# Residual additions on VectorE alone, modulation rows behind the products, and the first output granule by bank pairs

## The chip, the cores and the metric

One core of a Trainium2 chip runs the whole program in one launch. The metric is the time of one execution on the device, in microseconds (us). TensorE is written PE (matmuls) and PEld (weight loads), VectorE is DVE, ScalarE is ACT, GpSimd is POOL, and SyncE is SP.

## The reference, cut to what matters

Two blocks of two layers each work on 256 tokens of width 1024; everything is fp32. The first block also carries 256 context tokens beside the 256 latent ones. What the change touches is this part of the reference:

```python
def rms_norm(x, g):
    return x * lax.rsqrt(jnp.mean(x * x, axis=-1, keepdims=True) + EPS) * g

def swiglu(u, wi, wo):
    g, up = jnp.split(u @ wi, 2, axis=-1)
    return (jax.nn.silu(g) * up) @ wo
...
    m = (jax.nn.silu(c) @ w_ada + b_ada).reshape(c.shape[0], 1, N_MOD, D_MODEL)   # modulation, w_ada: 1024 x 9216 a layer
    mc = (jax.nn.silu(c_ctx) @ w_ada + b_ada).reshape(1, 1, N_MOD, D_MODEL)

    def pre(t, mm, i, gi):
        return rms_norm(t, g[gi]) * (1 + mm[:, :, i + 1]) + mm[:, :, i]

    def post(t, y, mm, i, gi, wres):
        return t + wres * mm[:, :, i + 2] * rms_norm(y, g[gi])
...
    h = post(h, swiglu(pre(h, m, 0, 0), ffn_wi[0], ffn_wo[0]), m, 0, 1, 0.5)      # first feed-forward
    h = post(h, o @ w_o, m, 3, 3, 1.0)                                            # mixer
    h = post(h, swiglu(pre(h, m, 6, 4), ffn_wi[1], ffn_wo[1]), m, 6, 5, 0.5)      # second feed-forward
# second block: x = x + _rmsnorm(mixer(...), g1);  x = x + _rmsnorm(_conv_ffn(_rmsnorm(x, g2), ...), g3)
```

## The kernel before, in words

Activations lie transposed: the model width is on the partitions, in 8 parts of 128 (`KD` = 8), and the tokens lie along the free axis, `T` = 512 (latent and context together) for most of the first block, 256 for the rest. `h[:, k, :]` is the residual stream of part k.

Every product is made from split operands: a weight tile is copied to its high part by ACT (L438), its low part is the difference, made by DVE (L443), and `multiply` (L445) issues three matmuls for each product (L452 to L454: high by high, high by low, low by high). Weights come through a ring of two 2 MB slots that SP loads (L408); one split step of 128 x 2048 is a granule, and there are two buffers each for the high and low parts.

The stages run one after another, each a block with one instruction list for each engine:

- `setup` (L497) loads the tokens, transposes them into `h`, loads six tiles of `w_ada` (1.5 MB each), multiplies them with the two conditioning vectors (`ada_rows`, L638, matmuls of L644), and makes the first norm's sum of squares. ACT squares each part of `h` (L623), and PE adds the eight with eight matmuls against a matrix of ones (L558), between the modulation tiles. The transposes of the vectors that are needed late (L565) stand at PE's end, and DVE's copies of them (L574) at DVE's end.
- `ffn1` (L1228), four times, is a feed-forward of 22 granules (`KF` = 22). `pair_products` (L1186) makes the gate and the value of granule g, 48 matmuls; ACT takes the gate (L1266), DVE multiplies (L1286) and so frees the banks, counted in `dve_free`. In the first two `ffn1` stages with a `w_ada` load (those of layer 0) the remaining 42 modulation tiles are made beside the products, one in a granule: class `Ada` (L667) loads a tile from ACT's queue into one single slot (L681), PE multiplies it (`Ada.rows`, L697), and only then can ACT issue the next load. `rows(0)` stands behind the first granule's products; for every later granule `rows(g)` stands in front of its products. The first stage has 22 such tiles, the second 20.
- `Down` (L1027) is the output product of the same feed-forward, 11 granules of 48 matmuls that add up in all eight PSUM banks. Granule 0 of it starts when its banks come free: before the first matmul into a bank, PE waits for the `dve_free` count of the granule whose gate or value lay there. The order is all eight banks for the first half of the granule (kk = 0), then all eight for the second (kk = 1). `ffn2` (L2069) uses the same `Down` behind a feed-forward with a short convolution, whose last step frees the banks (L2135).
- `Residual` (L877) with `Norm` (L731) is the border between two stages, ten times in all (one of them without a norm behind it). One matmul with ones gives the sum of squares of the new branch (L945), ACT makes 1/sqrt in `rstd` (L938, L939), DVE multiplies the eight parts with it (L954 where T is 512, L956 where T is 256), and the products are added to `h`: the odd parts by DVE (L961), the even ones by POOL (L966). ACT squares each new part (L771), PE sums the eight squares with eight matmuls with ones (L801), ACT makes the next `rstd` (L775, L776), DVE scales `h` (L807 or L809). Where T is 512 ACT then applies gain and shift in two instructions a part (L755, `make`) and copies the high part `uh` (L783), and DVE makes the low part `ul` (L816), which the first product waits for.

Each engine runs its list in order; a wait blocks all that is behind it on that engine.

Of the kernel before, what the change touches and what calls it, by code (L numbers as in the profile page):

```python
# [31 lines left out]
P = 128  # L32
D = 1024
# [126 lines left out]
def two_blocks(nc, a, out, stop=None):  # L160
    ctx = ExitStack()
    with ctx:
# [96 lines left out]
        def col(name, i, n=1):  # L259
# [17 lines left out]
        sum_ready, h_squared, h_updated, h_updated2, h_scaled, u_made, u_high, u_ready, gains = (signal(n) for n in (  # L277
            "norm_sum_ready", "h_squared", "h_updated_by_vector", "h_updated_by_gpsimd", "h_scaled", "input_made",
# [15 lines left out]
        first_loaded, late_loaded, tokens_loaded, const_loaded, gain_loaded, x_squared, x_summed = (signal(n) for n in (  # L294
            "first_vectors_loaded", "late_vectors_loaded", "tokens_loaded", "const_loaded", "gains_loaded", "x_squared", "x_summed"))
# [201 lines left out]
        def setup():  # L497
# [14 lines left out]
            SQUARES = {2: (0, 1), 3: (2, 3, 4), 4: (5, 6, 7)}  # L512
            TOKENS = {0: (0, 1, 2), 1: (3, 4, 5), 2: (6, 7)}

            with stage() as block:
# [18 lines left out]
                def _(pe):  # L534
# [8 lines left out]
                    for i in range(ADA_FIRST):  # L543
# [17 lines left out]
                    pe.wait_ge(late_loaded.sem, late_loaded.at(16 * len(late)))  # L561
                    for t in range(EARLY, len(row_tiles)):
                        g, m = KD + t, row_tiles[t]
                        turned(g)
                        pe.transpose(ps[:, bank_of(g), 0:m], rows[0:m, t, :], ident[0:m, 0:m]).then_inc(prod.sem, 1)  # L565

                @block.vector
                def _(dve):
# [9 lines left out]
                    for i in range(ADA_FIRST):  # L578
                        for j in TOKENS.get(i, ()):
                            g = EARLY + j  # L580
                            dve.wait_ge(prod.sem, prod.at(g + 1))
                            dve.tensor_copy(h[:, j, :], ps[:, bank_of(g), :]).then_inc(dve_free.sem, 1)
# [3 lines left out]
                    dve.wait_ge(gain_loaded.sem, gain_loaded.at(16 * 8))  # L586
                    dve.tensor_scalar(head_gain[:, 0::2], head_gain[:, 0::2], HD ** -0.5, None, ALU.mult)
                    for t in range(EARLY, len(row_tiles)):
                        take_cols(KD + t, t)

                @block.scalar
                def _(act):
# [21 lines left out]
                    for i in range(ADA_FIRST):  # L614
                        if i == ADA_FIRST - 1:
                            act.wait_ge(x_summed.sem, x_summed.at(KD))
                            act_chain.link(act, act.activation(rstd[:, :], ps[:, 7, :], ACT.Ln, scale=1.0 / D, bias=eps[:, 0:1]))
                            act.activation(rstd[:, :], rstd[:, :], ACT.Exp, scale=-0.5)
                        for k in SQUARES.get(i + 1, ()):
                            act.wait_ge(dve_free.sem, dve_free.at(EARLY + k + 1))  # L620
                            if k >= 4:
                                act.wait_ge(x_summed.sem, x_summed.at(k - 3))
                            act.activation(sq[:, k % 4, :], h[:, k, :], ACT.Square).then_inc(x_squared.sem, 1)  # L623
# [107 lines left out]
        class Norm:  # L731
# [26 lines left out]
            def scalar(self, act, high_of):  # L758
# [4 lines left out]
                else:  # L763
                    self.post.scalar(act)
                    for k in range(KD):

                        if k % 2:
                            act.wait_ge(h_updated.sem, h_updated.at(k // 2 + 1))
                        else:
                            act.wait_ge(h_updated2.sem, h_updated2.at(k // 2 + 1))  # L770
# [69 lines left out]

            def gpsimd(self, pool):
                if self.post is not None:
                    self.post.gpsimd(pool)
# [33 lines left out]
        class Residual:  # L877
# [69 lines left out]
            def vector(self, dve):  # L947
                T = self.T
                dve.wait_ge(y_rstd.sem, y_rstd.at(1))
                for k in range(KD):  # L950
# [8 lines left out]
                    if k % 2:  # L959
# [3 lines left out]
            def gpsimd(self, pool):  # L963
                for k in range(0, KD, 2):
                    pool.wait_ge(y_part.sem, y_part.at(k + 1))
# [32 lines left out]
        def residual(r):  # L998

            with stage() as block:  # L1000
# [12 lines left out]
                @block.gpsimd  # L1013
                def _(pool):
                    r.gpsimd(pool)
# [2068 lines left out]
```

## Time and profile before

| | |
|---|---|
| median of 3 runs | 3060.27 us (3059.58 to 3060.49) |
| the profiled execution's own time | 3062.88 us |
| its span | 3061.0 us |
| mean granted clock of TensorE over the span | 0.937 |
| busy: PE, PEld, DVE, ACT, POOL | 2780.4, 2356.8, 1342.7, 1176.4, 85.5 us |
| HBM read | 372.33 MB, 122 GB/s over the span |

The span runs from the first to the last instruction of the program in one profiled execution; 1.9 us of that execution lie outside it. An engine is busy while an instruction of it runs. The granted clock is 1.00 at full speed (2.4 GHz) and 0.50 at the lower level (1.2 GHz). In a row of the timeline "[4.62 <-ACT arena L771]" means that the engine had been idle for 4.62 us and that ACT's instruction of line 771 ended the wait.

### The profile page before, as it was taken

What the parts mean: (1) busy time and instruction counts of PE and PEld (TensorE: products, weight loads), DVE (VectorE), ACT (ScalarE), POOL (GpSimd) and SP (SyncE); (2) the same over time, 40 slices, a digit from 0 to 9 for tenths busy, and PEclk for the clock granted to TensorE, in tenths of its full rate; (3) what the DMA queues carried; (4) which work ended last, traced back from release to release, by engine and by line L of the source; (5) the groups of instructions that cost most, each with busy time, mean ns of one, the idle gap of its engine ahead of it and who ended that gap; (6) DMA issues with size and microseconds to landing.
All of it is one profiled execution on the core that took longest, in us unless ns stands there. A gap on an engine that the chain in (4) does not pass through costs nothing. (4 is left out here: it accounts for less than half of the span.)

```text
span 3061.0 us, 40121 instructions
## 1 busy us (share of the span) xinstructions
PE 2780.4 (91%) x16888; PEld 2356.8 (77%) x16888; DVE 1342.7 (44%) x1618; ACT 1176.4 (38%) x1581; POOL 85.5 (3%) x118
## 2 busy tenths in 40 slices
PE   5899998998999997999989899798896999777998
PEld 3677786875677785887868799798765899777998
DVE  3122236464222235222365644455445575444664
ACT  3122225444222225222254544343324464333653
POOL 3000000000000003000000000000000000000000
PEclk8899999999999998999999899899967899878899
DMA  8666321203566223232222355354000454331452
GB/s 278 197 206 206 145 95 63 77 29 103 185 212 213 101 98 86 82 110 82 96 83 62 105 165 177 115 190 142 1 1 28 138 190 154 117 106 56 138 171 104
DMA packets 277180, 375.54 MB, mean 123 GB/s; under 512 B 11020, under 2 KB 232696, under 8 KB 276912
## 3 DMA queue, kind: packets, MB, share of 16 engines
q1 hardware_dynamic: 228288, 300.56, 29.3%
q10 hardware_dynamic: 46576, 69.26, 6.7%
q0 software_dynamic: 2176, 3.67, 0.8%
q8 instruction: 109, 1.79, 0.2%
q14 instruction: 31, 0.25, 0.0%
HBM read 372.33 MB, written 1.16 MB: 122 GB/s over the span
## 5 line engine op out<-in xcount | busy, mean ns | idle before, releaser
L452 PE MATMUL ps<-uh,wh 128*128 128x256 f32 (+1 forms) x4224 | 1415.7, 335 | 70.7 <-DVE ul L816 31.0
L453 PE MATMUL ps<-ul,wh 128*128 128x256 f32 (+1 forms) x4224 | 1400.0, 331 | 0.0
L454 PE MATMUL ps<-uh,wl 128*128 128x256 f32 (+1 forms) x4224 | 1398.4, 331 | 0.0
L452 PEld LDWEIGHTS ps<-uh,wh 128*128 128x128 f32 x4224 | 813.5, 193 | 188.6 <-issue 82.3
L443 DVE TENSOR_TENSOR wl<-ring,wh 128x2048 fp32r<-128x2048 f32 x212 | 482.2, 2274 | 941.5 <-ACT wh L438 834.4
L454 PEld LDWEIGHTS ps<-uh,wl 128*128 128x128 f32 x4224 | 813.4, 193 | 72.8
L453 PEld LDWEIGHTS ps<-ul,wh 128*128 128x128 f32 x4224 | 814.0, 193 | 69.6 <-issue 0.7
L438 ACT ACTIVATE wh<-ring 128x2048 fp32r<-128x2048 f32 x156 | 298.4, 1913 | 803.7 <-PE ps L454 737.3
L1059 DVE TENSOR_TENSOR wl<-ring,wh 128x2048 fp32r<-128x2048 f32 x66 | 151.3, 2292 | 334.0 <-ACT uh L1077 296.9
L1056 ACT ACTIVATE wh<-ring 128x2048 fp32r<-128x2048 f32 x66 | 126.3, 1914 | 350.1 <-PE ps L454 350.1
L966 POOL TENSOR_TENSOR h<-h,arena 128x256 f32<-128x256 f32 (+1 forms) x40 | 43.7, 1093 | 2825.0 <-DVE arena L954 1441.4
L1478 ACT ACTIVATE wh<-ring 128x2048 fp32r<-128x2048 f32 (+2 forms) x38 | 70.0, 1842 | 125.9 <-PE ps L454 125.9
L801 PE MATMUL ps<-arena,const 128*128 128x256 f32 (+1 forms) x144 | 76.7, 699 | 38.7 <-ACT arena L771 38.7
L801 PEld LDWEIGHTS ps<-arena,const 128*128 128x128 f32 x144 | 39.0, 288 | 77.7 <-ACT arena L771 64.7
L644 PE MATMUL ps<-arena,act_c 128*32 128x384 f32 x736 | 72.8, 515 | 26.7 <-DMA arena<-in_w_ada_dram 26.7
L452 PE MATMUL ps<-wh,uh 128*128 128x256 f32 (+2 forms) x288 | 84.4, 293 | 0.0
L454 PE MATMUL ps<-wh,ul 128*128 128x256 f32 (+2 forms) x288 | 82.0, 285 | 0.0
L453 PE MATMUL ps<-wl,uh 128*128 128x256 f32 (+2 forms) x288 | 82.0, 285 | 0.0
L1084 DVE TENSOR_TENSOR ul<-arena,uh 128x1024 fp32r<-128x1024 f32 (+1 forms) x66 | 62.8, 952 | 28.1 <-ACT uh L1077 28.1
L1636 ACT ACTIVATE arena<-ps,softs 128x512 f32<-128x512 f32 (+1 forms) x72 | 43.6, 613 | 77.7 <-DVE softs L1675 62.6
L2152 DVE SCALAR_TENSOR_TENSOR arena<-ps,cols,arena 128x255 f32<-128x255 f32 x176 | 72.5, 473 | 0.0
L644 PEld LDWEIGHTS ps<-arena,act_c 128*32 128x32 f32 x736 | 19.9, 112 | 63.7 <-issue 50.8
(295 smaller groups left out, 2288.5 us busy)
## 6 DMA issues: line engine op xcount, KB each, us to landing
ring<-in_ffn_wi_dram SPq DMA_DIRECT2D x88, 1024.0 KB, 7.7
arena<-in_w_ada_dram ACTq DMA_DIRECT2D x42, 1536.0 KB, 6.6
ring<-in_ffn_w_up_dram SPq DMA_DIRECT2D x44, 1024.0 KB, 7.2
ring<-in_ffn_wo_dram SPq DMA_DIRECT2D x20, 2048.0 KB, 7.9
ring<-in_ab_w_in_dram SPq DMA_DIRECT2D x13, 2048.0 KB, 7.8
ring<-in_ffn_w_down_dram SPq DMA_DIRECT2D x10, 2048.0 KB, 7.8
ring<-in_c_w_in_dram SPq DMA_DIRECT2D x6, 2048.0 KB, 8.0
ring<-in_w_in_dram SPq DMA_DIRECT2D x20, 512.0 KB, 6.0
```

The lines of the kernel that those rows point to most:

```text
L438: act.activation(shape_of(wh[b]), raw, ACT.Copy).then_inc(high.sem, 1)
L443: dve.tensor_tensor(shape_of(wl[b]), raw, shape_of(wh[b]), ALU.subtract).then_inc(split.sem, 1)
L452: pe.matmul(to, sh, mh, start=start and n == 0, stop=False)
L453: pe.matmul(to, sh, ml, start=False, stop=False)
L454: mm = pe.matmul(to, sl, mh, start=False, stop=stop and last)
L644: last = pe.matmul(ps[q:q + 32, bank, 0:ADA_COLS], act_c[:, kk, ds(30 - 2 * r, 32)], weights[:, kk, :], start=(first and kk < 4), stop=(en ...
L801: last = pe.matmul(self.sum_bank(), ones, self.sq[:, k, :], start=(k == 0), stop=(k == KD - 1))
L1056: return act.activation(wh[side(self.key, g)][:, :], self.weights(g), ACT.Copy)
L1059: return dve.tensor_tensor(wl[side(self.key, g)][:, :], self.weights(g), wh[side(self.key, g)][:, :], ALU.subtract)
L1084: dve.tensor_tensor(to_l, of, to_h, ALU.subtract).then_inc(split.sem, 1)
L1478: act.activation(shaped(wh[side(key, g)]), raw, ACT.Copy).then_inc(high.sem, 1)
L2152: ins = dve.scalar_tensor_tensor(out=conv_buf[:, q, part, to], in0=ps[:, 2 * q + part, of], scalar=channel("ffn_conv_w", tap, part, g), in ...
```

## The change

Five edits, all in the order of work; no product, load or element-wise result is added or left out except where named.

1. `pair_products`: `rows(g)` moves behind the products of granule g. The tiles are shared out as 21 and 21 instead of 22 and 20, so that the last granule has none.
2. `Down.tensor`: every granule but the last goes by pairs of banks, both halves kk of a pair before the next pair; in granule 0 each pair waits once, before its first matmul.
3. `Residual` and `Norm`: POOL's four additions of each border go to DVE. DVE multiplies part k and then adds part k - 1.
4. `Norm.scalar`, T = 512: the high copy of part 0 is made before gain and shift of part 1.
5. `setup`: the eight squares are added by DVE (seven instructions of 128 x 512), and PE sums once; the late vectors are transposed and copied before the last modulation tile is done.

```diff
# setup
-                        for k in SQUARES.get(i, ()):
-                            if k == 0:
-                                pe.wait_ge(const_loaded.sem, const_loaded.at(16))
-                            pe.wait_ge(x_squared.sem, x_squared.at(k + 1))
-                            pe.matmul(ps[:, 7, :], ones, sq[:, k % 4, :], start=(k == 0), stop=(k == KD - 1)).then_inc(x_summed.sem, 1)
+                        if i == SUM_AFTER:      # 3
+                            pe.wait_ge(const_loaded.sem, const_loaded.at(16))
+                            pe.wait_ge(x_added.sem, x_added.at(KD - 1))
+                            pe.matmul(ps[:, 7, :], ones, sq_of(0), start=True, stop=True).then_inc(x_summed.sem, 1)
+                        if i == LATE_AFTER:     # 4
+                            pe.wait_ge(late_loaded.sem, late_loaded.at(16 * len(late)))
+                            for t in range(EARLY, len(row_tiles)):
+                                g, m = KD + t, row_tiles[t]
+                                turned(g)
+                                pe.transpose(ps[:, bank_of(g), 0:m], rows[0:m, t, :], ident[0:m, 0:m]).then_inc(prod.sem, 1)
...
+                    def add_square(k):
+                        dve.wait_ge(x_squared.sem, x_squared.at(k + 1))
+                        if k > 1:
+                            dve.wait_ge(x_added.sem, x_added.at(k - 1))
+                        dve.tensor_tensor(sq_of(0), sq_of(0), sq_of(k), ALU.add).then_inc(x_added.sem, 1)
+
+                    for j in range(KD):
+                        g = EARLY + j
+                        dve.wait_ge(prod.sem, prod.at(g + 1))
+                        dve.tensor_copy(h[:, j, :], ps[:, bank_of(g), :]).then_inc(dve_free.sem, 1)
+                        if j >= 2:
+                            add_square(j - 1)
+                    add_square(KD - 1)
+                    for t in range(EARLY, len(row_tiles)):
+                        take_cols(KD + t, t)
...
# Norm.scalar, T = 512
                     self.make(act, 0)
                     for k in range(KD):
-                        if k + 1 < KD:
+                        if 0 < k < KD - 1:
                             self.make(act, k + 1)
                         act.wait_ge(u_made.sem, u_made.at(2 * (k + 1)))
                         act.activation(uh[:, k, 0:T], self.made[:, k, :], ACT.Copy).then_inc(u_high.sem, 1)
+                        if k == 0:
+                            self.make(act, 1)
...
# Residual.vector (Residual.gpsimd and every block's POOL list with it are taken out)
-                    if k % 2:
-                        dve.wait_ge(y_part.sem, y_part.at(k + 1))
-                        dve.tensor_tensor(h[:, k, 0:T], h[:, k, 0:T], self.y[:, k, :], ALU.add).then_inc(h_updated.sem, 1)
+                    if k:
+                        self.update(dve, k - 1)
+                self.update(dve, KD - 1)
+
+            def update(self, dve, k):
+                dve.wait_ge(y_part.sem, y_part.at(k + 1))
+                dve.tensor_tensor(h[:, k, 0:self.T], h[:, k, 0:self.T], self.y[:, k, :], ALU.add).then_inc(h_updated.sem, 1)
...
# Down.tensor
-                left = {6: (dve_free, KF - 2), 0: (dve_free, KF - 1), 2: (dve_free, KF)}
-                order = (6, 7, 0, 1, 4, 5, 2, 3)
+                left = [((4, 5), dve_free, KF - 3), ((6, 7), dve_free, KF - 2), ((0, 1), dve_free, KF - 1), ((2, 3), dve_free, KF)]
                 if self.ada is not None:
-                    left, order = {0: (dve_free, KF - 1), 2: (dve_free, KF), 6: (ada_summed, 2)}, (4, 5, 0, 1, 2, 3, 6, 7)
+                    left = [((4, 5), ada_copied, 2), ((0, 1), dve_free, KF - 1), ((2, 3), dve_free, KF), ((6, 7), ada_summed, 2)]
...
-                        for kk in range(2):
-                            for j in order:
-                                if g == 0 and kk == 0 and j in left:
-                                    sem, count = left[j]
-                                    pe.wait_ge(sem.sem, sem.at(count))
-                                c = slice(kk * D + j * P, kk * D + (j + 1) * P)
-                                last = multiply(pe, ps[:, j, 0:self.T], [((vh[:, c], vl[:, c]), (xh[:, kk, :], xl[:, kk, :]))],
-                                                start=(g == 0 and kk == 0), stop=False)
+                        for banks, free, count in left:
+                            if g == 0:
+                                pe.wait_ge(free.sem, free.at(count))
+                            for kk in range(2):
+                                for j in banks:
+                                    c = slice(kk * D + j * P, kk * D + (j + 1) * P)
+                                    last = multiply(pe, ps[:, j, 0:self.T], [((vh[:, c], vl[:, c]), (xh[:, kk, :], xl[:, kk, :]))],
+                                                    start=(g == 0 and kk == 0), stop=False)
...
# pair_products
                 pe.wait_ge(free.sem, free.at(g + 1 - pairs))
-                if ada is not None:
-                    ada.rows(pe, g)
...
                 last.then_inc(prod.sem, 1)
+                if ada is not None:
+                    ada.rows(pe, g)
...
-        adas = {(0, 0): Ada(tiles[:KF]), (0, 1): Ada(tiles[KF:])}
+        adas = {(0, 0): Ada(tiles[:KF - 1]), (0, 1): Ada(tiles[KF - 1:])}
```

## Rows read from the trace of the kernel before

**Rows 1.** The page's first part, busy time of each engine.
```profile
PE 2780.4 (91%) x16888; PEld 2356.8 (77%) x16888; DVE 1342.7 (44%) x1618; ACT 1176.4 (38%) x1581; POOL 85.5 (3%) x118
```

**Rows 2.** Waits of PE, whole span: line waited for: us in total, times, longest.
```profile
PE ps L801 <- ACT arena L771: 38.7, 20, 4.6
...
PE ps L644 <- DMA arena<-in_w_ada_dram: 26.7, 3, 15.5
...
PE ps L452 <- DVE arena L2135: 8.6, 2, 4.3
...
PE ps L452 <- DVE arena L1286: 2.2, 3, 1.3
```

**Rows 3.** Timeline of PE, both stages with modulation rows: start, us, instruction [idle before].
```profile
87.37 2.79 PE L644 MATMUL ps<-arena,act_c 128*32 128x384 f32 x16 [15.47 <-DMA arena<-in_w_ada_dram]
...
102.71 1.50 PE L644 MATMUL ps<-arena,act_c 128*32 128x384 f32 x16
...
115.28 1.50 PE L644 MATMUL ps<-arena,act_c 128*32 128x384 f32 x16
...
772.13 2.79 PE L644 MATMUL ps<-arena,act_c 128*32 128x384 f32 x16 [6.80 <-DMA arena<-in_w_ada_dram]
...
786.49 1.50 PE L644 MATMUL ps<-arena,act_c 128*32 128x384 f32 x16
```

**Rows 4.** Timeline of ACT, then line L681's landing times to 100 us and after 85 us.
```profile
72.10 0.40 ACTq L681 DMA_DIRECT2D arena<-in_w_ada_dram  x1
...
DMA to landing us min/median/max: 6.7/10.7/15.1
...
DMA to landing us min/median/max: 6.3/6.6/7.4
```

**Rows 5.** Timeline of PE and of DVE where the first second-block output product starts.
```profile
2555.41 0.58 PE L452 MATMUL ps<-uh,wh 128*128 128x256 f32 x1 [4.32 <-DVE arena L2135]
...
2554.94 0.99 DVE L2135 TENSOR_TENSOR arena<-arena 128x256 f32<-128x256 f32 x2
```

**Rows 6.** Busy time by stretch there: length, PE, PEld, DVE, ACT, POOL, granted clock, DMA.
```profile
2554.40:2561.10 6.70, 5.69 (x26) 5.70 (x27) 2.07 (x5) 2.33 (x3) 0.00 (x0) 0.50 0.28 70
2561.20:2568.00 6.80, 6.80 (x59) 6.80 (x59) 2.23 (x2) 2.44 (x2) 0.00 (x0) 1.00 0.58 235
```

**Rows 7.** Timeline of DVE, POOL, ACT, PE at the 484 us border, T = 512.
```profile
483.80 1.29 DVE L954 TENSOR_TENSOR arena<-arena,rstd 128x512 f32<-128x512 f32 x2 [2.20 <-ACT rstd L939]
485.13 1.63 DVE L961 TENSOR_TENSOR h<-h,arena 128x512 f32<-128x512 f32 x1
...
498.96 1.89 DVE L807 TENSOR_TENSOR arena<-h,rstd 128x512 f32<-128x512 f32 x3 [1.37 <-ACT rstd L776]
...
493.20 1.65 POOL L966 TENSOR_TENSOR h<-h,arena 128x512 f32<-128x512 f32 x1 [1.23 <-DVE arena L954]
...
494.87 1.18 ACT L771 ACTIVATE arena<-h 128x512 f32<-128x512 f32 x2 [1.70 <-POOL h L966]
...
486.93 8.29 PE L801 MATMUL ps<-arena,const 128*128 128x512 f32 x12 [4.62 <-ACT arena L771]
495.56 1.98 PE L801 MATMUL ps<-arena,const 128*128 128x512 f32 x4 [0.33 <-ACT arena L771]
```

**Rows 8.** Busy time by stretch in the same border, columns as in Rows 6.
```profile
492.00:494.00 2.00, 2.00 (x5) 1.07 (x5) 1.97 (x4) 1.18 (x3) 0.80 (x1) 0.83 0.00 0
```

**Rows 9.** Timeline of PE at the 1737 us border, T = 256.
```profile
1741.74 4.20 PE L801 MATMUL ps<-arena,const 128*128 128x256 f32 x10 [0.66 <-ACT arena L771]
```

**Rows 10.** Timeline of ACT and of PE behind the 731 us border, T = 512.
```profile
748.87 0.62 ACT L783 ACTIVATE uh<-arena 128x512 fp32r<-128x512 f32 x1
...
750.35 0.77 PE L452 MATMUL ps<-uh,wh 128*128 128x512 f32 x1 [5.61 <-DVE ul L816]
```

**Rows 11.** Timeline of DVE and of ACT at the end of setup.
```profile
48.61 1.08 DVE L574 COPY cols<-ps 128x128 f32<-128x128 f32 x5
...
50.82 1.91 ACT L438 ACTIVATE wh<-ring 128x2048 fp32r<-128x2048 f32 x1 [3.62 <-DMA ring<-in_ffn_wi_dram]
```

More of the change, by code:

```diff
@@ L275, in two_blocks @@
         aux = signal("second_dve_step")
-        sum_ready, h_squared, h_updated, h_updated2, h_scaled, u_made, u_high, u_ready, gains = (signal(n) for n in (
-            "norm_sum_ready", "h_squared", "h_updated_by_vector", "h_updated_by_gpsimd", "h_scaled", "input_made",
+        sum_ready, h_squared, h_updated, h_scaled, u_made, u_high, u_ready, gains = (signal(n) for n in (
+            "norm_sum_ready", "h_squared", "h_updated", "h_scaled", "input_made",
             "input_high_parts", "input_ready", "gains_ready"))
@@ L293, in two_blocks @@
             "ada_tile_loaded", "ada_tile_multiplied", "ada_rows_copied", "ada_columns_made", "ada_columns_summed", "ada_columns_taken"))
-        first_loaded, late_loaded, tokens_loaded, const_loaded, gain_loaded, x_squared, x_summed = (signal(n) for n in (
-            "first_vectors_loaded", "late_vectors_loaded", "tokens_loaded", "const_loaded", "gains_loaded", "x_squared", "x_summed"))
+        first_loaded, late_loaded, tokens_loaded, const_loaded, gain_loaded, x_squared, x_added, x_summed = (signal(n) for n in (
+            "first_vectors_loaded", "late_vectors_loaded", "tokens_loaded", "const_loaded", "gains_loaded", "x_squared", "x_squares_added", "x_summed"))
         ada_ready = [signal(f"ada_tile{i}_loaded") for i in range(ADA_FIRST)]
@@ L511, in setup @@
             bank_of = lambda g: 4 + g % 3
-            SQUARES = {2: (0, 1), 3: (2, 3, 4), 4: (5, 6, 7)}
+            SUM_AFTER, LATE_AFTER = 3, 4
+            sq_of = lambda k: sq[:, 1 + (k - 1) % 3, :] if k else sq[:, 0, :]
             TOKENS = {0: (0, 1, 2), 1: (3, 4, 5), 2: (6, 7)}
@@ L577, in _ @@
                         take_cols(t, t)
[L578 to L582, printed above, removed]
+                    def add_square(k):
[12 more added lines that the diff above has]
+                        take_cols(KD + t, t)
+                    dve.wait_ge(gain_loaded.sem, gain_loaded.at(16 * 8))
+                    dve.tensor_scalar(head_gain[:, 0::2], head_gain[:, 0::2], HD ** -0.5, None, ALU.mult)
                     dve.wait_ge(ada_turned.sem, ada_turned.at(1))
@@ L585, in _ @@
                     ada_take(dve, mod_sums, 0, ADA_FIRST).then_inc(ada_taken.sem, 1)
[L586 to L589, printed above, removed]
                 @block.scalar
@@ L613, in _ @@
                     act.preload_act_table_set(LN_EXP)
[L614 to L623, printed above, removed]
+                    for k in range(KD):
+                        act.wait_ge(dve_free.sem, dve_free.at(EARLY + k + 1))
+                        if k >= 4:
+                            act.wait_ge(x_added.sem, x_added.at(k - 3))
+                        act.activation(sq_of(k), h[:, k, :], ACT.Square).then_inc(x_squared.sem, 1)
+                    act.wait_ge(x_summed.sem, x_summed.at(1))
+                    act_chain.link(act, act.activation(rstd[:, :], ps[:, 7, :], ACT.Ln, scale=1.0 / D, bias=eps[:, 0:1]))
+                    act.activation(rstd[:, :], rstd[:, :], ACT.Exp, scale=-0.5)
                     act.wait_ge(ada_multiplied.sem, ada_multiplied.at(ADA_FIRST))
@@ L958, in vector @@
                     ins.then_inc(y_part.sem, 1)
-                    if k % 2:
-                        dve.wait_ge(y_part.sem, y_part.at(k + 1))
-                        dve.tensor_tensor(h[:, k, 0:T], h[:, k, 0:T], self.y[:, k, :], ALU.add).then_inc(h_updated.sem, 1)
-            def gpsimd(self, pool):
-                for k in range(0, KD, 2):
-                    pool.wait_ge(y_part.sem, y_part.at(k + 1))
-                    pool.tensor_tensor(h[:, k, 0:self.T], h[:, k, 0:self.T], self.y[:, k, :], ALU.add).then_inc(h_updated2.sem, 1)
-                pool.wait_ge(h_updated2.sem, h_updated2.at(KD // 2))
+                    if k:
[4 more added lines that the diff above has]
+                dve.tensor_tensor(h[:, k, 0:self.T], h[:, k, 0:self.T], self.y[:, k, :], ALU.add).then_inc(h_updated.sem, 1)
             def tail_done(self):
@@ L979, in done @@
                 y_part.passed(KD)
[L980 to L981 removed]
+                h_updated.passed(KD)
         def residual1(l, i, gi, weight, T=T2):
@@ L1296, in _ @@
                 def _(pool):
-                    norm.gpsimd(pool)
                     if bands_of is not None:
@@ L1487, in _ @@
                     steps(split_one, lambda g: take(dve, 1, dve_free, g), beside.vector(dve) if beside else lambda g: None)
-                @block.gpsimd
-                def _(pool):
-                    norm.gpsimd(pool)
             norm.done()
@@ L1746, in _ @@
                         stream(sp, out_key)
-                @block.gpsimd
-                def _(pool):
-                    norm.gpsimd(pool)
                 @block.tensor
@@ L2163, in _ @@
                     down.vector(dve)
-                @block.gpsimd
-                def _(pool):
-                    norm.gpsimd(pool)
             norm.done()
```

17 lines of the change are left out of this document (1 added, 16 removed).

## The prediction

> **What bounds the kernel now.** I read the busy times first. PE is busy for 2780 of 3061 us [rows 1], and every product and load stays, so the change can only give back part of the 281 us in which PE idles, and what PE loses at the lower clock behind such idle time. Next, the waits of PE by releaser, to see which idle time the five edits touch [rows 2]: 38.7 us before the sums of squares (L801), 26.7 us for modulation tiles, 8.6 us and 2.2 us before banks at the start of `Down`. Then the timeline at each of these places. PE is the only engine that is never covered there, so a microsecond won on PE's list is one won of the end.
>
> **Edit 1, rows behind the products.** In the first stage PE waits 15.47 us, from 71.90 to 87.37, for tile 1; in the second 6.80 us [rows 3]. The cause is the order: ACT can issue load 1 only behind `rows(0)`, at 72.10, it lands 15.1 us later (the longest of the three loads to 100 us) [rows 4], and `rows(1)` stands next on PE with nothing between. After the change granule 1's 48 matmuls stand between. One granule with its rows is 12.57 us (102.71 to 115.28) and the rows are about 1.45 of it, so the products are 11.1 us. Load 1 is issued as before and should land at 87.2; PE does products until 83.0 and waits 4.3 us: 11.1 us less. The clock comes on top: from `rows(1)` to `rows(2)` PE took 15.34 us instead of 12.57, 2.8 us lost; in the second stage 14.36, 1.8 lost [rows 3], each behind its wait. I charge the 4.3 us that stay with the 1.8 us that the 6.80 us wait cost. First stage: 11.1 + 2.8 - 1.8 = 12.1. Second stage: the load has 11.1 us of cover for a wait of 6.80, so 6.8 + 1.8 = 8.6. Together **20.7 us** (18 if the clock gives nothing back and load 1 comes no later; 22.5 if the short wait costs no clock). Moving a tile from the first stage to the second is 1.45 us from one to the other.
>
> What is queued behind the new wait: ACT waits for `rows(g)`, then issues the next load, splits granule g + 2 (1.9 us), takes the gate of g (0.6); DVE makes the low part (2.3 us). Granule g + 2 starts 11.1 + 1.45 us behind `rows(g)`, and the chain is under 5 us (L438's 1.91 us as in [rows 11]), so 7 us are free. Load g + 1 has 11.1 us of cover, as before, and takes 6.6 us, 7.4 at most [rows 4].
>
> **Edit 2, `Down` by pairs.** Before, PE did 6 matmuls (banks 6 and 7, first half) and waited 4.32 us for bank 0, freed by DVE's second last product (L2135) [rows 5]; there are two such waits [rows 2]. Now banks 4, 5, 6 and 7 are free already and give 24 matmuls before that wait. 18 matmuls at 0.12 us (59 in 6.80 us [rows 6]) move into the idle time: 2.1 us. Behind the wait the granted clock was 0.50 for 6.8 us and 26 matmuls took 5.7 us, 2.7 more than at full clock [rows 6]. The idle time shrinks to 2.2 us, so I expect the fall to be gone in most cases, and take 4.0 each, **8.0** for two (4.2 to 9.6). What is late next is the low part of granule 1's input, behind the second L2135 of the pair that ends at 2555.9 [rows 5], one ACT table load and one copy, an estimated 2 us: about 2558, just when granule 0 now ends (2555.4 and 24 matmuls). The three waits for L1286, 2.2 us, go whole [rows 2]: where T is 512 there are 12 more matmuls (0.23 us each) of cover for 0.4 us, where T is 256 there are 18 more for 1.3 us. **2.2**. The later granules change only the order of banks: 0.
>
> **Edit 3, additions on DVE.** At the 484 us border, T = 512, DVE's multiplications go in 1.29 us a pair, and its addition takes 1.63 us; the last POOL addition ends at 494.85, ACT squares two parts behind it, and PE's last two sums end at 497.54 [rows 7]. On one engine it is 16 instructions. The trace has no such addition without POOL beside it. From below it is L807 (h by rstd, both from SBUF), three in 1.89 us, 0.605 each; from above the 1.63 us itself. I take 0.605: the same shape and operands, and the 1.63 us end 0.55 us behind POOL's. Then part 6 is added at 483.80 + 14 x 0.605 + 0.68 = 492.95 and part 7 at 493.56, squared by 494.2 instead of 496.05: 1.9 us earlier. PE's sums may be later: they start at 486.4 instead of 486.93, the clock is at half until about 492.7 (0.83 over 492 to 494 [rows 8]), a part costs about 1.75 us at half and 0.9 at full clock, so 3.6 parts and then 4.4 x 0.9 gives 496.7: 0.9 us gained. The four borders with T = 512 lie between 0.9 and 1.9 each, according to when the clock rises; 1.4 on the mean, **5.6** (2 to 9, if the clock rises earlier or later).
>
> The Trainium skill (SBUF — State Buffer, section Who interferes with whom) says that a VectorE instruction with two SBUF inputs and a GpSimd instruction that reads SBUF exclude each other, the later one blocked until the first ends. That reads the 1.63 us as about 1.0 of waiting and 0.6 of work, and the sum by it is the 5.6 above; if the 1.63 were the addition's own price, the sum would be that of rival E.
>
> At T = 256 I count **0** (-1.5 to 1.5 over the five): PE's last five parts take 4.20 us without a break [rows 9], PE is the pace, and ACT's split of a granule stands between parts 2 and 3 as before. The last border, without a norm, ends with DVE's sixteenth instruction either way: 0.
>
> **Edit 4, first high part.** `uh` of part 0 starts at 748.87 behind four `make` instructions and PE's first product at 750.35 [rows 10]. Two of the four now stand behind it, 1.0 us earlier. The later parts come no sooner, since ACT's work is the same, and PE is at half clock there, so about half of it counts: 0.45 at two borders, **0.9** (0 to 2). Where PE has other work in the gap (the two `latent` borders) and at setup, where DVE splits weights first: 0.
>
> **Edit 5, setup.** The five copies of the late vectors, 1.08 us, leave DVE's end. But ACT's first split waited for its ring tile until 50.82 (3.62 us idle, released by the DMA) [rows 11], which neither PE nor DVE can bring sooner. **0** (-1, if the modulation load issued earlier takes from the ring tile; +1.4).
>
> **Sum.** 20.7 + 8.0 + 2.2 + 5.6 + 0.9 = 37.4 us off the profiled execution's own 3062.9 us (3061.0 span and 1.9 around it) gives 3025.5. The median of the runs is 2.6 us below that execution: **3023 us**. Where each of some 25 falls of the clock lies against the work will shift too, which I estimate at 4 us either way.
>
> **Rivals.**
> A, the forecast: 3023, chance 0.56.
> B, the waits shrink but the clock does not come back. For it: a wait of about 4.3 us stays in the first stage and one of 2.2 us in each `ffn2`, and the borders still have 4 to 6 us of idle PE. Against: both behind-wait losses are tied to longer waits. Idle time alone, 11.1 + 6.8 + 4.2 + 2.2, and 3.6 and 0.4 at the borders, is 28.3: about 3032, 0.16.
> C, more than forecast: the clock also rises sooner in the borders, and setup gives its microsecond. Upper bounds 22.5 + 9.6 + 2.2 + 9 + 2 + 1.4 = 46.7: about 3014, 0.12.
> D, load 1 hides less. It took 15.1 us where later ones took 6.6, so DMA was crowded; if more requests move into that stretch and it lands 5 us later, with rows(2) waiting too, the first stage gives 0 to 5: about 3034, 0.06.
> E, the addition itself costs 1.57: 8 x 0.605 + 8 x 1.57 = 17.4 us, DVE ends at 501.2, PE at 502.7 instead of 497.5, 5.2 lost at four borders instead of 5.6 won: 3023 + 5.6 + 21 = 3050, 0.03.
> F, slower. The place is every granule of the two modulation stages: ACT's split and load now wait for the end of PE's granule, not for its start. If the load behind that wait took what load 1 took, 15.1 us against 11.1 of cover, PE would idle 4 us in 40 granules, 160 us: about 3180. It decides from a mean excess of 0.9 us a granule, a load of 12.0 us. Against: 6.6 and 7.4 at most [rows 4]. 0.04.
> Little effect (within 0.2%, 6 us, about what a measurement of this kernel can tell from no change), several terms at their low ends: 0.03.
>
> So faster 0.93, same 0.03, slower 0.04. The range, 3012 to 3040, takes in A to D.
>
> **What would show it.** L644 waits for DMA in the first stage for 3 to 6 us and in the second not at all; rows(1) to rows(2) near 12.6 us. L2135 as PE's releaser falls from 8.6 to about 4.4 us, with the granted clock at 1.00 behind; L1286 is gone. The addition by DVE lasts 0.68 us at T = 512, and L801's last pair follows its predecessor without idle time. The first product at 50 to 57 us starts at the same time. Wrong would be: an idle PE in granules 2 to 20 of the modulation stages, released by wl or by L644's load; additions over 1 us; a first `Down` granule that waits for `ul` longer than before.

## The result, and the profile after

| | before | after |
|---|---|---|
| median of the runs | 3059.93 us (4 runs) | 3021.65 us (4 runs, 3019.8 to 3026.5) |
| ratio, 95% interval | | 0.9876 [0.9863, 0.9888] |
| profiled execution, span | 3062.88, 3061.0 us | 3022.63, 3020.9 us |
| PE idle in the span | 280.6 us | 257.1 us |
| PE busy at granted clock 0.50 | 243.0 us | 219.4 us |

38 us went, against 37.4 in the prediction's sum. PE's idle time fell by 23.5 us; its busy time fell by 16.6, of which 11.8 is half of the 23.6 us less at the lower clock, and the rest is mainly the seven sums that edit 5 takes off PE. Taken at the end of the last product before each of the ten borders, the lead over the kernel before grows like this: 13.8, 14.1, 24.9, 26.0, 27.4, 28.0, 28.7, 33.4, 35.3, 40.1 us. Four steps make nearly all of it: the two modulation stages (13.8 and 10.8) and the two second-block feed-forwards (4.7 and 4.8).

The line numbers move: L644 is L651 now, L681 L688, L801 L807, L816 L822, L961 L967, L954 L956, L771 L775, L1084 L1079 and L2135 L2122. PE's waits in the changed kernel (who waited for whom, total, times, longest) answer to [rows 2]; L1286's wait has no row any more. Of the five waits for modulation tiles only one, of 5.40 us, lies in the modulation stages; the other four, 10.7 us in all with the longest of 6.2, lie in setup, where such waits took 4.4 us before:

```profile
PE ps L807 <- ACT arena L775: 33.8, 16, 4.1
...
PE ps L651 <- DMA arena<-in_w_ada_dram: 16.1, 5, 6.2
...
PE ps L452 <- DVE arena L2122: 4.3, 2, 2.2
```

The timeline of PE in the two modulation stages, after (start, us, instruction, idle before), answers to [rows 3]:

```profile
87.81 2.79 PE L651 MATMUL ps<-arena,act_c 128*32 128x384 f32 x16 [5.40 <-DMA arena<-in_w_ada_dram]
...
102.29 1.50 PE L651 MATMUL ps<-arena,act_c 128*32 128x384 f32 x16
...
746.45 1.50 PE L651 MATMUL ps<-arena,act_c 128*32 128x384 f32 x16
...
759.02 1.50 PE L651 MATMUL ps<-arena,act_c 128*32 128x384 f32 x16
...
771.59 1.50 PE L651 MATMUL ps<-arena,act_c 128*32 128x384 f32 x16
```

The first stage's wait is 5.40 instead of 15.47 us; behind it the rows still take 2.79 us, at the lower clock, and from there to the next rows PE takes 14.48 us (87.81 to 102.29), not the 12.57 of a granule without a wait. In the second stage the rows follow each other at 12.57 us with no wait at all. The landing time of that one load, issued at 71.5 us, answers to [rows 4]:

```profile
DMA to landing us min/median/max: 16.3/16.3/16.3
```

Where the first second-block output product starts, the timeline of PE answers to [rows 5]:

```profile
2524.21 0.28 PE L454 MATMUL ps<-uh,wl 128*128 128x256 f32 x1
2526.65 0.39 PE L452 MATMUL ps<-uh,wh 128*128 128x256 f32 x1 [2.16 <-DVE arena L2122]
```

and the busy time by stretch (length, then PE, PEld, DVE, ACT, POOL, granted clock, DMA) to [rows 6]:

```profile
2521.90:2528.60 6.70, 4.54 (x38) 4.33 (x37) 4.61 (x7) 3.97 (x7) 0.00 (x0) 1.00 0.00 0
```

The wait is halved (2.17 us at the second such place) and the granted clock stays at 1.00 behind it, at both places.

At the first border with T = 512, the timelines of DVE, ACT and PE, after, answer to [rows 7]:

```profile
472.20 0.68 DVE L967 TENSOR_TENSOR h<-h,arena 128x512 f32<-128x512 f32 x1
...
479.42 1.29 DVE L967 TENSOR_TENSOR h<-h,arena 128x512 f32<-128x512 f32 x2
480.63 2.28 DVE L443 TENSOR_TENSOR wl<-ring,wh 128x2048 fp32r<-128x2048 f32 x1
```

```profile
480.14 1.23 ACT L775 ACTIVATE arena<-h 128x512 f32<-128x512 f32 x2 [0.57 <-DVE h L967]
482.93 0.69 ACT L779 ACTIVATE rstd<-ps,eps 128x512 f32<-128x512 f32 x1 [1.55 <-PE ps L807]
```

```profile
473.60 9.29 PE L807 MATMUL ps<-arena,const 128*128 128x512 f32 x16 [4.11 <-ACT arena L775]
```

An addition takes 0.68 us now (1.63 before). PE sums all eight parts without a break in 9.29 us; the squares are ready at 481.37, 1.5 us before the sum is. PE is the pace.

### The profile page after: what moved, and what is told of

It is laid out like the page before. It is cut to its first block and busy times, and to the rows that moved or that the text cites. A ratio compares the mean times of both kernels' runs of the same rounds, so it can differ in the third digit from the quotient of the medians.

```text
span 3020.9 us, 40097 instructions
## 1 busy us (share of the span) xinstructions
PE 2763.8 (91%) x16874; PEld 2346.1 (78%) x16874; DVE 1340.8 (44%) x1665; ACT 1178.3 (39%) x1581; POOL 41.8 (1%) x78
## 5 line engine op out<-in xcount | busy, mean ns | idle before, releaser
L453 PEld LDWEIGHTS ps<-ul,wh 128*128 128x128 f32 x4224 | 811.8, 192 | 69.1 <-issue 0.7
L807 PE MATMUL ps<-arena,const 128*128 128x256 f32 (+1 forms) x144 | 74.4, 686 | 33.8 <-ACT arena L775 33.8
L807 PEld LDWEIGHTS ps<-arena,const 128*128 128x128 f32 x144 | 39.1, 285 | 70.7 <-ACT arena L775 60.0
L651 PE MATMUL ps<-arena,act_c 128*32 128x384 f32 x736 | 72.8, 515 | 16.1 <-DMA arena<-in_w_ada_dram 16.1
L1079 DVE TENSOR_TENSOR ul<-arena,uh 128x1024 fp32r<-128x1024 f32 (+1 forms) x66 | 62.9, 952 | 27.1 <-ACT uh L1072 27.1
L1072 ACT ACTIVATE uh<-arena 128x1024 fp32r<-128x1024 f32 (+1 forms) x66 | 54.7, 828 | 33.1 <-PE ps L454 33.0
L438 ACT ACT_TABLE_LOAD x26 | 33.4, 1283 | 72.1 <-PE ps L651 71.8
```

The source lines that it names most:

```text
L438: act.activation(shape_of(wh[b]), raw, ACT.Copy).then_inc(high.sem, 1)
L453: pe.matmul(to, sh, ml, start=False, stop=False)
L651: last = pe.matmul(ps[q:q + 32, bank, 0:ADA_COLS], act_c[:, kk, ds(30 - 2 * r, 32)], weights[:, kk, :], start=(first and kk < 4), stop=(en ...
L807: last = pe.matmul(self.sum_bank(), ones, self.sq[:, k, :], start=(k == 0), stop=(k == KD - 1))
L1079: dve.tensor_tensor(to_l, of, to_h, ALU.subtract).then_inc(split.sem, 1)
```

## The experiments

Times in this section are medians; each group was timed beside the kernel before on its own chip, where that kernel took 3060.7, 3062.3 and 3059.3 us. The changed kernel run again in the second group took 3019.5 us (ratio 0.9858 [0.9842, 0.9875]). Since the times of one kernel spread over 2 to 13 us, I read the effects below from the profiles: the lag or lead at the end of the last product before each border. Each of these is the difference of two single executions. The changed kernel has two profiles, of 3020.9 and 3018.0 us: edits 1, 2 and 3 undone are held against the first, edits 4 and 5 undone against the second, which ran beside them.

**Edit 1 undone.**

```diff
                 pe.wait_ge(free.sem, free.at(g + 1 - pairs))
+                if ada is not None:
+                    ada.rows(pe, g)
...
-                if ada is not None:
-                    ada.rows(pe, g)
...
-        adas = {(0, 0): Ada(tiles[:KF - 1]), (0, 1): Ada(tiles[KF - 1:])}
+        adas = {(0, 0): Ada(tiles[:KF]), (0, 1): Ada(tiles[KF:])}
```

> The changed kernel with edit 1 alone undone: the modulation rows stand before their granule's products again, 22 and 20 tiles. Theory (the wait for tile 1 was uncovered, and the clock fell behind it): PE waits about 15.5 us in the first modulation stage and about 6.8 us in the second, the second granule's stretch from rows(1) to rows(2) is 15.3 and 14.4 us instead of 12.6, and the kernel takes 18 to 21 us more than the changed one, about 3041 us. Rival (the gain came from the other edits or from a luckier fall of the clock): under 10 us more, below 3032 us.

3039.2 us, ratio 0.9927 [0.9914, 0.9940]. The span is 19.1 us longer than the changed kernel's: 11.7 us behind the first modulation stage and 8.4 behind the second, 20.0 in all, and about that stays to the end. The medians differ by 17.6 us: this profile is of the slowest of the kernel's six runs. PE's longest wait for a tile is 16.7 us again:

```profile
PE ps L651 <- DMA arena<-in_w_ada_dram: 33.3, 6, 16.7
```

**Edit 1 alone**, on the kernel before.

> The kernel before with edit 1 alone. Theory (edit 1 is independent of the others): the wait for tile 1 falls from 15.5 to about 5 us, that of the second stage goes, 19 to 21 us less than the kernel before, about 3041 us. Rival (edit 1 pays only because edits 3 and 4 bring PE to its first granules sooner): under 12 us less, above 3048 us.

3041.75 us, ratio 0.9943 [0.9929, 0.9957]; the span is 21.0 us shorter, 11.3 to 12.4 by the first stage and 6.4 by the second; the rest came later, without any edit there (below). So edit 1 is worth 17.7 us in its two stages without the other edits and 20.0 with them, and does not hang on them.

**Edit 2 undone.**

```diff
...
-                        for banks, free, count in left:
-                            if g == 0:
-                                pe.wait_ge(free.sem, free.at(count))
-                            for kk in range(2):
-                                for j in banks:
+                        for kk in range(2):
+                            for j in order:
+                                if g == 0 and kk == 0 and j in left:
+                                    sem, count = left[j]
+                                    pe.wait_ge(sem.sem, sem.at(count))
```

> The changed kernel with edit 2 alone undone: Down goes through all eight banks for each half again. Theory: the two second-block feed-forwards wait 4.3 us for L2135's product instead of 2.2 and run the next 6.8 us at a granted clock of 0.50, 4.7 us each; the three waits for the first block's product come back with 2.2 us in all; about 11.5 us more than the changed kernel, 3033 us. Rival (only the idle time counts, the clock falls either way): 2 x 2.1 + 2.2 = 6.4 us more, 3028 us.

3037.3 us, ratio 0.9924 [0.9910, 0.9938]; the span is 14.6 us longer, the median 15.7. The two second-block feed-forwards lose 4.7 and 4.8 us, as the first theory has it. Three of the first-block ones lose 0.9, 1.8 and 0.6; the waits that come back there are 2.2 us in all, so that about 1 us of these 3.3 is of the clock. In the undone kernel the wait is back, and the first matmul behind it takes 0.58 us instead of 0.39:

```profile
2530.17 0.58 PE L452 MATMUL ps<-uh,wh 128*128 128x256 f32 x1 [4.33 <-DVE arena L2123]
```

A further 1.9 us arise where no code differs, between 2620 and 2830 us of the kernel before, in the stretch treated at the end. Three smaller shifts, -1.7, +0.8 and +1.1 us, nearly cancel; the first of them is a fall of the clock that the changed kernel's first profile has and this one has not.

**Edit 3 undone.** POOL makes every second addition.

```diff
-                    if k:
-                        self.update(dve, k - 1)
-                self.update(dve, KD - 1)
+                    if k % 2:
+                        dve.wait_ge(y_part.sem, y_part.at(k + 1))
+                        dve.tensor_tensor(h[:, k, 0:T], h[:, k, 0:T], self.y[:, k, :], ALU.add).then_inc(h_updated.sem, 1)
...
+                for k in range(0, KD, 2):
+                    pool.wait_ge(y_part.sem, y_part.at(k + 1))
+                    pool.tensor_tensor(h[:, k, 0:self.T], h[:, k, 0:self.T], self.y[:, k, :], ALU.add).then_inc(h_updated2.sem, 1)
```

> The changed kernel with edit 3 alone undone: POOL makes every second residual addition again. Theory as predicted (1.4 us gained at each border with T = 512): 5.6 us more, 3027 us. Theory after the traces (PE sums eight parts without a break at the half clock, and behind the sum ACT sets the pace in the latent stages, so that little of an earlier start is kept there): the sums end 0.9 to 1.4 us later at each of four borders, but the end only 2 to 5 us later, 3024 to 3026 us. Rival (DVE loses at T = 256 what it wins at T = 512): within 1 us of the changed kernel, 3021 us.

3025.3 us, ratio 0.9878 [0.9862, 0.9895]; the span is 4.1 us longer. At each of the four borders with T = 512 the sum ends 1.3 us later against its own start; with what the clock adds, the kernel is 7.8 us behind after the fourth. At the next border, T = 256, it wins 2.2 us back in the sums alone (6.0 us for them instead of 8.2), and 1 more up to the next. Nothing of the edit is in those sums: in the changed kernel the granted clock was 0.50 there without a break, from 1703 to 1727 us:

```profile
1703.00:1727.00 24.00, 14.27 (x44) 11.03 (x45) 17.89 (x38) 11.96 (x24) 0.00 (x0) 0.50 0.28 88
```

So edit 3 is worth 5 us (four times 1.3) in the sums themselves, 6.1 if each is counted from the branch's sum before it (1.3, 1.9, 1.6 and 1.3), up to 7.8 with the clock that goes with it, and the clock gave part of that back later by chance. The whole time alone would not show the edit: the medians differ by 3.6 us, and the ratios to the kernel before are 0.9878 and 0.9876.

With POOL back, the addition takes what it took before. The first addition of each engine at this border, DVE's and POOL's, edit 3 undone:

```profile
472.39 1.63 DVE L970 TENSOR_TENSOR h<-h,arena 128x512 f32<-128x512 f32 x1
...
471.84 1.64 POOL L975 TENSOR_TENSOR h<-h,arena 128x512 f32<-128x512 f32 x1 [395.86 <-DVE arena L963]
```

DVE's ends 0.54 us behind POOL's.

**Edit 4 undone.**

```diff
                     for k in range(KD):
-                        if 0 < k < KD - 1:
+                        if k + 1 < KD:
                             self.make(act, k + 1)
...
-                        if k == 0:
-                            self.make(act, 1)
```

> The changed kernel with edit 4 alone undone (ACT makes parts 0 and 1 before the first high part). Theory: the first product starts 0.9 us later at the four borders with T = 512, half of it counts where PE is at the half clock (two borders) and nothing where ACT sets the pace (two): about 0.9 us more than the changed kernel, 3022.5 us, within the noise of the times but to be read from the profile. Rival (all of it counts): 3 to 4 us more, 3025 us.

3021.7 us, ratio 0.9867 [0.9851, 0.9884], 2.2 us above the changed kernel beside it; the profile is 3.0 longer. The first product starts 0.8 us later at each border with T = 512. Of this nothing is left by the next border after the latent stage at 484 us (1.22 behind at the first product, 0.19 at 713 us), and about half of it is left behind the 731 us one (1.00, then 0.67, of which 0.2 were there before). That is the theory, shown at one of its two borders. Behind the other, between 1159 and 1525 us, 3.3 us appear. There the granted clock stays at 0.50 until 1164.4 us, 3.4 us longer than in the changed kernel beside it, and falls to 0.50 for another 3.4 us at 1403 us, which together make up the 3.3 us. The changed kernel's first profile has the second of these falls too (last section), so I count the edit at about 0.5 us where it is shown and 1 us if the other border gives as much; whether the first of the two falls is its doing is open.

**Edit 5 undone.** Setup as before.

> The changed kernel with edit 5 alone undone (setup as before). Theory: setup ends with the ring tile's landing either way; the first product starts at 56.4 instead of 56.5 us and the time is within 1 us of the changed kernel, 3021 us. Rival (the shorter list of DVE was worth the 1.1 us of its five copies): first product at 57.5 us.

3016.5 us, ratio 0.9862 [0.9844, 0.9879]; the profile is 5.2 us shorter than the changed kernel's beside it, the medians 3.0. That it is faster is not shown: its runs lie between 3014.5 and 3026.3 us, and the changed kernel's ratio beside it is 0.9858, lower than this one. The first product starts at 56.6 us in it and at 56.5 and 56.0 in the changed kernel's two profiles: setup's length is set by the DMA, as the theory says. But setup with edit 5 leaves PE idle while it waits for the last modulation tile, and the clock can fall. Timeline of PE at the end of setup, first the changed kernel:

```profile
44.94 2.79 PE L651 MATMUL ps<-arena,act_c 128*32 128x384 f32 x16 [2.75 <-DMA arena<-in_w_ada_dram]
48.33 0.90 PE L658 MATMUL ps<-const,arena 128*128 128x128 f32 x3 [0.61 <-ACT arena L632]
56.52 0.77 PE L452 MATMUL ps<-uh,wh 128*128 128x512 f32 x1 [7.29 <-DVE ul L822]
```

and with edit 5 undone:

```profile
42.80 2.84 PE L558 MATMUL ps<-arena,const 128*128 128x512 f32 x6
45.58 1.50 PE L644 MATMUL ps<-arena,act_c 128*32 128x384 f32 x16
47.68 0.55 PE L651 MATMUL ps<-const,arena 128*128 128x128 f32 x3 [0.61 <-ACT arena L625]
...
56.59 0.77 PE L452 MATMUL ps<-uh,wh 128*128 128x512 f32 x1 [6.71 <-DVE ul L815]
```

The same sixteen matmuls take 2.79 us behind 2.75 us of idle time and 1.50 us behind the sums. But with the changed kernel's setup, the kernel with edit 1 undone kept the clock behind nearly the same idle time:

```profile
44.81 1.50 PE L651 MATMUL ps<-arena,act_c 128*32 128x384 f32 x16 [2.59 <-DMA arena<-in_w_ada_dram]
```

The first granule's products end at 69.9 us in the changed kernel and at 69.3 with edit 5 undone. This 0.6 us is no cost of the edit. The modulation rows behind those products start at 70.4 us in the kernel before, 70.3 with edit 1 alone and 69.2 with edit 5 undone, all three with setup as before; with edit 5 at 69.8, 69.8, 69.1 (edit 1 undone) and 70.4 (edit 3 undone). The start goes with the moment at which the granted clock rises in the first granule: 59.9 us in the two early ones, 61.2 to 62.6 us in the others. The remaining 4.5 us of difference come mainly in two jumps of 2.2 in the sums at T = 256, again from where the clock stood. So no worth or cost of edit 5 is shown.

**The band transfers moved.** In the first feed-forward POOL issues 27 small transfers for the latent stage's position bands, 24 of them from 61 to 76 us and three before. Here they wait for the last modulation tile:

```diff
+            if ada is not None:
+                pool.wait_ge(ada_multiplied.sem, ada_multiplied.at(ada.n))
```

> The changed kernel, but GpSimd's transfers of the position bands in the first feed-forward (25 small issues, 50 to 76 us before) start only after the last modulation tile has been multiplied. Theory (the second modulation tile takes 16 us to land because it shares the DMA engines with the band transfers and one ring tile): without the bands it lands in 8 to 11 us, by 83 us, the wait of 5.4 us falls to 0 to 1 and the clock does not fall behind it: 6 to 8 us less than the changed kernel, 3014 to 3016 us. Rival (the ring tile's 2 MB alone make it late): the landing time stays at 14 us or more and the time within 2 us of the changed kernel.

3014.3 us, ratio 0.9849 [0.9834, 0.9864]. The load of tile 1 lands after 11.4 us instead of 16.3, PE waits 0.47 us for it, and the clock does not fall. The load's landing, PE's timeline and the busy time by stretch show it:

```profile
DMA to landing us min/median/max: 11.4/11.4/11.4
```

```profile
81.81 1.50 PE L651 MATMUL ps<-arena,act_c 128*32 128x384 f32 x16 [0.47 <-DMA arena<-in_w_ada_dram]
```

```profile
81.00:90.00 9.00, 8.53 (x48) 6.02 (x47) 2.89 (x2) 2.40 (x2) 0.00 (x0) 1.00 0.57 179
```

The lead over the changed kernel is 7.9 us at the first border and 8.3 at the end (5.5 against its second profile, which won 2.9 us elsewhere): 4.9 us of wait saved, 1.1 us by which the first rows happened to start earlier, and 1.9 us of clock. So the bands made the load 4.9 us later, and that cost 6.8 us. In a quiet stretch such a load lands after 6.6 us; what holds this one for the other 4.8 us no run separates.

**Fillers at the borders.** To test whether the lower clock makes the sums slow (`FILL` is 12):

```diff
                 self.post.tensor(pe)
+                if self.T == T2:
+                    for _ in range(FILL):
+                        pe.matmul(ps[:, 1, 0:P], ones, ones, start=True, stop=True)
```

> The changed kernel with twelve extra 128 x 128 matmuls of ones on PE, into a bank that the next sum clears, between the branch's sum and the first square at the four borders with T = 512 (results are not touched). They fill the 4.1 us in which PE idles. Theory (the eight sums are slow, 9.3 us in all, because the clock is at half after that idle time): the clock rises about 3.4 us earlier, the sums end 1 to 2 us sooner, 3 to 6 us less than the changed kernel, 3016 us. Rival (the sums wait for ACT's squares anyway, or the fillers delay them): within 1 us or up to 4 us more, 3021 to 3025 us.

3020.4 us, ratio 0.9867 [0.9851, 0.9883], 0.9 above the changed kernel beside it. The clock rises at 472.2 us, against 478.2 in the changed kernel beside it. But the first of the four sums takes 8.9 instead of 9.3 us (first profile) and the other three 9.3 as before, and counted from the branch's sum the first ends after 15.4 us, as before. The timeline of PE with fillers:

```profile
466.12 2.05 PE L951 MATMUL ps<-arena,const 128*128 128x512 f32 x2 [4.05 <-PEq L1234]
467.96 4.86 PE L808 MATMUL ps<-const 128*128 128x128 f32 x24
472.66 3.15 PE L811 MATMUL ps<-arena,const 128*128 128x512 f32 x6
477.00 4.56 PE L811 MATMUL ps<-arena,const 128*128 128x512 f32 x10 [1.19 <-ACT arena L776]
```

Part 3's square comes late, since ACT splits a granule (1.89 us) between parts 2 and 3, and five parts at 0.91 us remain. At the lower clock PE is the pace, at the higher one ACT's list is, and both end at the same time. My theory was right on the clock and wrong on its worth: the rival, that the sums wait for ACT's squares, holds.

**ACT's split later, where T is 256.**

```diff
-                        if k == 2:
+                        if k == (2 if T == T2 else 5):
                             high_of(1)
```

> The changed kernel, but where T is 256 ACT splits the next granule's weights behind part 5 of the squares instead of behind part 2 (five borders). Theory (at T = 256 neither DVE nor POOL sets the end of the sums: PE sums parts of 0.85 us at the half clock, and the only break in them is ACT's split of 1.9 us): the break of 0.65 us and the late parts behind it go, the sums end 1.0 to 1.3 us earlier at each border, 4 to 6 us less than the changed kernel, 3015 us. Rival (the additions on DVE set the pace at T = 256, edit 3 cost there what it won at T = 512): the sums end at the same time, 3020 us.

3022.3 us, ratio 0.9880 [0.9865, 0.9895]: no gain. Locally the theory holds: at each of the five borders the sum ends 1.2 to 1.3 us sooner after its start (6.87 instead of 8.19 us at the fifth border). But of 6.5 us in all only 2.2 are left against the changed kernel's first profile: this kernel is 1.9 us behind at the last product before the first of the five (the fifth border of the ten) and 0.3 ahead at the end. The losses lie between the borders, 0.1 to 1.8 us each, where nothing was edited, and there the clock has falls that the changed kernel does not, as at 2526 us, behind PE's waits of 1.4 and 2.2 us that both kernels have (busy time by stretch, this kernel; the changed kernel has 1.00 there):

```profile
2526.30:2529.50 3.20, 3.20 (x17) 3.20 (x17) 0.69 (x1) 0.72 (x2) 0.00 (x0) 0.50 0.20 32
```

**The best version.** The changed kernel with setup as before, the bands moved, and the later split.

> The changed kernel without edit 5 (setup as before), with the band transfers behind the last modulation tile and with ACT's split behind part 5 where T is 256. Theory: the three gains add up, 8.3 for the bands, 1 for setup, 5 for the split: about 3006 us. Rival (the clock's falls take back part of it): 3010 to 3014 us.

3009.15 us (3008.1 to 3013.7), ratio 0.9837 [0.9823, 0.9850] to the kernel before. It beats both kernels. Its profile is only 0.6 us shorter than that with the bands alone, but it is of the slowest of its five runs; its median is 5.1 us lower (ratios 0.9837 and 0.9849 to the kernel before on two chips, with intervals that overlap). So the bands are what is shown to matter, and whether the other two add anything is open.

## Why the prediction was right

The forecast of 3023 us and its steps against what was measured:

- Edit 1, 20.7 us: measured 20.0 over its two stages by undoing it (19.1 in the span, 17.6 in the medians) and 17.7 over them when alone. The mechanism is as stated, the clock's loss behind the wait that stays included: 14.48 us from those rows to the next against 12.57, so 1.9 us where the sum charges 1.8. The sign "rows(1) to rows(2) near 12.6 us" did not come; it contradicted that charge. The first stage gave 11.7 instead of 12.1, since load 1 landed after 16.3 us instead of 15.1; the second 8.4 (8.6). Rival F has nothing for it: no granule from 2 on waits.
- Edit 2, 8.0 and 2.2 us: 9.5 in the second block, since the clock stayed up both times where I had taken it for probable, and 3.3 against 2.2 in the first. The 1.9 us more between 2620 and 2830 us had no term.
- Edit 3, 5.6 us at T = 512 and 0 at T = 256: 1.3 us of sum a border, 5.2 in all (6.1 counted from the branch's sums), 4.1 in the span. The price of 0.605 us a step for an addition was right (2 in 1.29 us), and rival E is refuted. PE became the pace, as I had bounded it.
- The Trainium skill's rule (SBUF — State Buffer, section Who interferes with whom) is borne out: without GpSimd beside it the same addition takes 0.68 instead of 1.63 us, and with GpSimd back it takes 1.63 us again and ends 0.54 us behind GpSimd's.
- Edit 4, 0.9 us: about 0.5 at one of the two borders that I named; at the other the clock hides it.
- Edit 5, 0 us: nothing else is shown. The first product starts within 0.4 us of where it did, as said. The prediction did not ask what PE's clock does in setup's new waits; it fell in some profiles and not in others.
- The 4 us for falls of the clock that move: of the right size. It is why the sum of the undone edits (19.1 + 14.6 + 4.1 + 3.0 - 5.2 = 35.6) does not come out at 40.1, the difference of the two spans. All five against the first profile give 29.8, against the second, where that difference is 43.0, 44.3.

So the mechanisms and the sizes of edits 1 to 3, over nine tenths of the sum, are shown. That the median came within 1.4 us of the forecast is partly luck: two profiles of the changed kernel alone differ by 2.9 us, and edit 1 gave less and edit 2 more than its term.

Rival B was wrong for edits 1 (second stage) and 2 and right for the wait that stayed in the first stage: its rows ran at the lower clock.

## What to carry to other kernels

When the load behind a single buffer can only be issued after the buffer's last use, put the next use behind the longest piece of independent work, and look at what else is loading at that time: here 27 small transfers made one load 5 us later and cost 7. A wait of PE costs its length and then what the clock loses behind it (1.8 us for a wait of 6.8, 2.5 for one of 4.3), so shortening a wait enough to keep the clock is worth more than what is taken off the wait. An edit that wins about 1 us in a place can't be judged by the time of such a kernel: read it from the profile, look at more than one profile before you call a microsecond its doing, and expect the clock to move as much elsewhere.

## What was not expected of the hardware

Two profiles of the same changed kernel agree within 0.1 us at every border up to 1133 us and then differ by 1.7 us by 1523 us (2.9 at the end). In one of them the granted clock falls for 3.4 us in a full stretch of products, which accounts for the 1.7 us. The busy time by stretch, first the first profile, then the second:

```profile
1402.70:1406.00 3.30, 3.30 (x10) 2.56 (x9) 3.00 (x3) 1.73 (x2) 0.00 (x0) 0.50 0.00 0
```

```profile
1402.70:1406.00 3.30, 3.30 (x16) 2.73 (x15) 2.90 (x3) 1.63 (x2) 0.00 (x0) 1.00 0.00 0
```

The short idle time ahead of it (2.4 us before `Down`) is the same in both, so such an idle time does not by itself decide whether the clock falls behind it; what does is open. The stretch between 2620 and 2830 us has the same effect between kernels: the 60 us around the gated linear attention's start have a mean granted clock of 0.72 in the kernel before and with edit 2 undone, and 0.77 in the changed kernel, and these two lose 1.9 us there. No edit touches that stretch, yet the loss is not random: all three kernels without edit 2 (that with edit 1 alone too) lose 1.8 to 1.9 us against the changed one and have the clock at 0.50 for 30.7 us on end there, and the changed kernel's two profiles have 23.9 us. The two kernels with the later split, which have edit 2, have 30.7 us too. So it goes by what happened before, and how is open. The rows of the kernel before and of the changed kernel:

```profile
2700.00:2760.00 60.00, 44.11 (x270) 38.65 (x269) 28.50 (x45) 20.49 (x26) 0.67 (x3) 0.72 0.21 72
```

```profile
2667.00:2727.00 60.00, 43.89 (x292) 39.11 (x291) 30.42 (x49) 20.69 (x26) 0.67 (x3) 0.77 0.21 73
```
